# The transposes of a head's probabilities, one score tile later in the written order of attention

## The reference

```python
logits = [einsum('bqkgd,bskd->bkgqs', qi, ki) * scale for qi, ki in zip(qblk, ks)]
p = softmax(concatenate(logits))          # windowed heads: one sink logit more in the denominator
out = einsum('bkgqs,bskd->bqkgd', p, v)   # over latent keys and 128 past keys
```

## Time and profile before

| | us |
|---|---|
| median of 3 runs | 1852.12 (1851.22 to 1853.79) |
| the profiled execution | 1850.76 |
| its span, first to last instruction | 1849.0 |
| PE busy | 1738.5 (94%) |
| DVE busy | 1112.3 (60%) |
| ACT busy | 638.6 (35%) |
| attention of layer 0 | about 181 to 418 us of the span |
| attention of layer 1 | about 1082 to 1304 us of the span |

### The profile page before, as it was taken

One profiled execution on the slowest core, in us unless ns is written; L12 is line 12 of the kernel. 1 busy time (PEld: TensorE's weight loads), 2 busy tenths in 40 slices (PEclk: granted clock), 3 DMA queues, 4 the chain that ended last, 5 costly groups with the idle time before them and its releaser, 6 DMA issues.

```text
span 1849.0 us, 30546 instructions
## 1 busy us (share of the span) xinstructions
PE 1738.5 (94%) x11801; PEld 1563.9 (85%) x11801; DVE 1112.3 (60%) x2272; ACT 638.6 (35%) x1302; POOL 149.4 (8%) x152
## 2 busy tenths in 40 slices
PE   6999888889999999999999988879999999999997
PEld 4898555459999999999989965545899999999997
DVE  3656655554775656565772856656467665656575
ACT  2421553453432222223243235435344222222223
POOL 0351010101000000000003402010200000000000
PEclk7899999899999999999999999999999999999999
DMA  7431432233122222222222322202313222222221
GB/s 267 115 94 40 150 109 90 88 114 103 47 92 80 68 79 68 79 68 80 76 66 65 92 76 92 92 23 92 92 58 92 81 68 79 68 77 70 80 58 58
DMA packets 188441, 156.56 MB, mean 85 GB/s; under 512 B 7825, under 2 KB 175285, under 8 KB 188341
## 3 DMA queue, kind: packets, MB, share of 16 engines
q1 hardware_dynamic: 188340, 155.19, 27.4%
HBM read 151.86 MB, written 3.31 MB: 84 GB/s over the span
## 4 chain that ended last, share of the span: by engine, by line
PE 85%; DVE 7%; ACT 3%; issue 2%; DMA 1%; POOL 1%; SPq 0%; DVEq 0%; ACTq 0%
PE PS L1112 81%; PE PS L1116 5%; DVE QTR L1573 1%; DVE H_lo L1630 1%; POOL SS L764 1%; DVE H_lo L1876 1%; ACT PR L951 1%; DVE PR L1849 1%; DVE ST L1830 1%; ACT H_hi L783 1%; DMA RW<-in_w_in_dram 1%; DMA RW<-in_w_ada_dram 1%; DVE X L1679 0%; POOL W_lo L742 0%; ACT PT L783 0%
## 5 line engine op out<-in xcount | busy, mean ns | idle before, releaser
L1112 PE MATMUL PS<-H_hi,W_hi 128*128 128x384 f32 (+1 forms) x1728 | 416.6, 310 | 0.0
L1112 PE MATMUL PS<-H_hi,W_lo 128*128 128x384 f32 (+1 forms) x1728 | 416.5, 310 | 0.0
L1112 PE MATMUL PS<-H_lo,W_hi 128*128 128x384 f32 (+1 forms) x1728 | 416.5, 310 | 0.0
L1112 PEld LDWEIGHTS PS<-H_lo,W_hi 128*128 128x128 f32 x1728 | 275.7, 189 | 0.0
L1112 PEld LDWEIGHTS PS<-H_hi,W_lo 128*128 128x128 f32 x1728 | 275.5, 189 | 0.0
L1112 PEld LDWEIGHTS PS<-H_hi,W_hi 128*128 128x128 f32 x1728 | 274.5, 189 | 0.8 <-issue 0.8
L783 ACT ACTIVATE W_hi<-RW 128x1024 fp32r<-128x1024 f32 (+1 forms) x176 | 184.0, 1050 | 172.3 <-PE PS L1112 161.6
L1945 DVE TENSOR_SCALAR CF<-U,VT 128x644 f32<-128x644 f32 x88 | 48.9, 556 | 268.8 <-ACT U L783 268.6
L1112 PE MATMUL PS<-G_hi,W_hi 128*128 128x384 f32 (+1 forms) x704 | 171.5, 310 | 0.0
L1112 PE MATMUL PS<-G_lo,W_hi 128*128 128x384 f32 (+1 forms) x704 | 171.0, 309 | 0.0
L1112 PE MATMUL PS<-G_hi,W_lo 128*128 128x384 f32 (+1 forms) x704 | 170.8, 309 | 0.0
(11 more groups left out here) (168 smaller groups left out, 2467.7 us busy)
## 6 DMA issues: line engine op xcount, KB each, us to landing
RW<-in_w_ada_dram SPq DMA_DIRECT2D x96, 512.0 KB, 4.4
RW<-in_w_up_dram SPq DMA_DIRECT2D x88, 512.0 KB, 3.7
RW<-in_w_down_dram SPq DMA_DIRECT2D x44, 512.0 KB, 3.6
RW<-in_w_in_dram SPq DMA_DIRECT2D x28, 512.0 KB, 3.8
RW<-in_w_out_dram SPq DMA_DIRECT2D x16, 512.0 KB, 3.5
RW<-in_w_in_dram SPq DMA_DIRECT2D x8, 352.0 KB, 3.0
out_dram<-OUT SPq DMA_DIRECT2D x5, 512.0 KB, 2.9
XIN<-in_x_sample_dram SPq DMA_DIRECT2D x4, 512.0 KB, 6.4
```

What stands on the lines that cost most here:

```text
L1112: return nc.tensor.matmul(out, lhsT, rhs, start=start, stop=stop, skip_group_check=True)
```

## The change

Only the list changes. In the order of before, T("P",h,5) stood ahead of S(h+1,0), and the step T("P",h,k) behind S(h+1,k). Now T("P",h,5) stands behind S(h+1,0), T("P",h,k) behind S(h+1,k+1), and T("P",h,4), which no score tile is left for, behind the last SEL of the head, ahead of the next K or Q. The values follow: V(h,3) stands behind K, V(h,4) behind Q.

```diff
@@ -189,21 +189,22 @@
     for h in range(HEADS):
         t, v = probs(h - 1) if h else ([], [])
         if h == 8:
-            order += t[:1] + late + t[1:2]
+            order += late + t[:2]
             for x in range(2, len(t)):
                 order += v[x - 2:x - 1] + t[x:x + 1]
             order += v[-2:]
             t, v, late = [], [], []
+        order += late[:1]
         if h == 0 or kv_of(h) != kv_of(h - 1):
             order += [("T", ("K", kv_of(h), 0)), ("T", ("K", kv_of(h), 1))]
-        order += late + [("T", ("Q", h, 0)), ("T", ("Q", h, 1))]
+        order += late[1:2] + [("T", ("Q", h, 0)), ("T", ("Q", h, 1))] + late[2:]
         if h == 3:
             order.append(("PREP", 1))
         todo = [chunks.pop(0) for _ in range(1 + (len(chunks) > HEADS - h if h % 3 == 0 else len(chunks) >= 2 * (HEADS - h)))]
-        order += [("ADA", todo[0])] + t[:1]
+        order += [("ADA", todo[0])]
         for q in range(NQ):
             order.append(("S", h, q))
-            order += t[q + 1:q + 2] + v[q:q + 1]
+            order += t[q:q + 1] + (v[q - 1:q] if q else [])
             if q == 0:
                 order.append(("MOVE", todo[0]))
             if q == 1:
@@ -212,7 +213,7 @@
                 order += mla[3 * q:3 * q + 3]
             if q == 3 and len(todo) > 1:
                 order.append(("ADA", todo[1]))
-        late = v[5:]
+        late = t[5:] + v[4:]
         if len(todo) > 1:
             order += [("MOVE", todo[1]), ("SEL", todo[1])]
         if h == 7:
```

## The result

| | median us | runs | ratio to before, 95% |
|---|---|---|---|
| before, beside this set | 1852.95 (1851.22 to 1855.04) | 4 | |
| changed | 1870.34 (1867.35 to 1871.79) | 4 | 1.0091 (1.0074 to 1.0109) |
| changed, second set (experiment 5) | 1866.50 (1861.59 to 1867.41) | 4 | 1.0058 (1.0042 to 1.0075) |

The sign was right. The size was not: forecast 1862 with 1855 to 1869, and the first set lies above that range. The second set lies in it, and the two intervals hardly touch. So the question behind the result was what differs between executions of the same instructions. The chip of the first set is not on record, so a difference between chips is not ruled out; but the kernel before, on three chips, has means of 1855.0, 1855.8 and 1855.2, and the second set, on one chip, spreads over 5.8 us by itself.

What follows compares the result with a forecast made beforehand. PE was taken to bound the kernel (85% of the chain), so its idle time in attention counts in full. 9.6 + 1.6 - 1.0 = +10.2 us on the median of 1852.12 gave 1862, range 1855 to 1869.

Steps and rivals of the forecast that it cites:

- part 1: Ten head changes a layer: PE's wait for T("P",h,5) moves behind S(h+1,0), 31.2 us against 21.6 before, +9.6 us.
- the upper bound: Wait behind S(h+1,0): PE's first transpose after idle time or POOL's work beside DVE adds 0.3 us, so +15.5.
- part 2: T("P",h,4) behind SEL: K's second part waits 0.2 us for ACT's move at eight places, +1.6 us (0 to 2.5).
- part 3: Heads 7 to 8: T("P",6,4) and V(6,3) fill idle time, -0.5 us a layer, -1.0 in both (-2 to +1).
- The static sum: Whole kernel, without TensorE's clock: 9.6 + 1.6 - 1.0 = +10.2 us.
- TensorE's clock is left out of the sum: No clock loss counted, though one more dip at each of heads 0 to 1 and 8 to 9 would be +5.6 us.
- windows around a head start with a clock below 1: Sign of being wrong: around head starts TensorE is granted less than its full 2.4 GHz; no size given.
- the clock falls at every head: Rival: 20 clock dips of 1.4 us at head changes come on top, 1889 us; chance 0.07.
- The rival with the wait gone: DVE normalises (h,4) ahead of the new head's maximum, so all 21.6 us of wait are saved: 1831 us; chance 0.07.

Runs made afterwards that it cites:

- experiment 5: The changed kernel run again with only a comment altered, for a second set of runs and a second profile: median 1866.50 us, ratio 1.0058.
- Experiment 1: Changed kernel, but DVE normalises the old head's last tile before taking the new head's first maximum: median 1829.55 us, ratio 0.9865.
- experiment 2: Kernel before with only T("P",h,5) moved behind S(h+1,0), all other transposes and values left in place: median 1891.53 us, ratio 1.0205.
- experiments 7 and 11: Kernel of experiment 6 plus twelve unread matmuls in PE's waits between heads 7 and 8, run in two sets: medians 1822.59 and 1819.73 us.
- experiment 6: Kernel of Experiment 1 with T("P",h,4) ahead of the head's last SEL, except in head 7: median 1829.60 us, ratio 0.9863.
- second pair: Kernels of Experiment 1 and experiment 6, each run again on one chip: medians 1832.01 and 1828.41 us.

## Why the prediction was right or wrong

**Right, part 1.** That DVE takes the new maximum first and PE waits 1.59 us behind S(h+1,0) is measured to the hundredth: 1.59, 1.39 from head 3 to 4, 1.57 to 1.58 for windowed heads, against 1.59, 1.39 and 1.57. The 0.3 us more of the upper bound came at no place. The ten places of a layer sum to 19.8 - 2.2 - 1.95 = 15.65 (15.6 forecast). S(h+1,0) starts without a wait for `QTR`. Experiment 1 shows that this order on DVE is the cause, experiment 2 that moving T("P",h,5) alone brings it.

**Right, part 2.** K's second part waits 0.25 us at four places of a layer, 2.0 in both (1.6 forecast). SEL's wait is unchanged.

**Wrong, part 3.** The -0.5 us a layer did not come. PE's waits between heads 7 and 8 are 0.87 + 2.22 + 0.22 = 3.3 us in layer 0 and 1.31 + 2.20 + 0.22 = 3.7 in layer 1, against 2.49 + 0.48 + 0.23 = 3.2 and 2.65 + 0.94 + 0.22 = 3.8 before; in the second profile they are 3.6 and 3.8. So the term of -1.0 was in fact 0 to +0.3. Lines of the changed kernel's first profile, in both layers:

```profile
336.12 0.65 PE L1113 MATMUL PS<-PT,PMS 128*64 128x256 f32 x2 [0.87 <-ACT PT L784]
340.21 0.69 PE L1113 MATMUL PS<-PT,PMS 128*64 128x128 f32 x2
...
1239.65 0.65 PE L1113 MATMUL PS<-PT,PMS 128*64 128x256 f32 x2 [1.31 <-ACT PT L784]
1242.50 1.30 PE L1117 MATMUL PS<-K,PR 128*128 128x128 f32 x5 [2.20 <-DVE PR L1850]
```

Two of the kernel before, in layer 1:

```profile
1223.89 0.30 PE L1116 MATMUL PS<-K,PR 128*128 128x128 f32 x1 [2.65 <-DVE PR L1849]
...
1226.29 0.66 PE L1112 MATMUL PS<-PT,PMS 128*64 128x128 f32 x2 [0.94 <-DVE H_lo L1876]
```

V(7,5) starts 5.98 us after the last MLA product in layer 0 (340.21 - 334.23), where the five transposes ahead of it took 1.30 us, and 5.41 in the second profile, where they took 0.74: about the 5.3 to 5.9 forecast. In layer 1 it is 6.4 in both, as PE waits 1.3 us there for ACT's move before V(6,4). Besides, the first profile lost 5.1 us of clock in the 16 us from 336 on; the profile of before lost 3.4 in the 16 us from 328 on, the same place.

**Wrong: the clock, and a range too narrow for it.** The static sum was 10.2 and came out 12.1: part 3 is 1.0 to 1.3 of the difference, part 2 is 0.4, part 1 is 0.1. That alone would have left the result in the range. With the first set's mean of 1870.0 the forecast of 1862 misses 8. Of this 1.9 is the static part. 3.3 is the base: 1852.1 came from three runs, and 26 later runs of the kernel before have a mean of 1855.4. 2.2 is clock, 49.1 us lost in the first set against a mean of 46.9 before (in the second set it was 45.2). The 0.6 left over is rounding and the spread of the estimates. The 3.3 is probably clock as well: the profiled run of the base lost 40.7 us, the 26 lost 46.9 on average; the clocks of the two other runs of the base are not on record. So the failed step is "TensorE's clock is left out of the sum", with 3.7 us as what a measurement can tell and 1869 as the upper end. The eight runs of the changed kernel lie between 1861.6 and 1871.8, 10 us apart by where their clock falls, and the base was one execution at 0.978 and two more quick ones. On average the change cost no clock (47.1 us lost against 46.9), so the second set, at 1866.5, falls inside the range; which set came first was luck. Why the clock falls at a place in one execution and not in another stays open.

One of the prediction's signs of being wrong did appear: windows around a head start with a clock below 1, as at heads 0 to 1 of layer 0, 0.64 and 0.73 in the two profiles of the changed kernel. The rival "the clock falls at every head" did not happen in the changed kernel; experiment 2, with two waits around one tile, comes nearest to it. The rule of the Trainium skill ("TensorE: Matmul & The Clock Gate", Part 1) that recent activity sets the clock agrees with experiments 7 and 11. The unequal outcome of equal waits in the two profiles above, and experiment 6, with less idle time and less clock, are not explained by it alone.

The rival with the wait gone has its time from an order that the change did not make; experiment 1 made it: 1829.55 and 1832.01, where 1831 was worked out. The mechanism was as described, but the closeness is in part luck: at full clock 18.7 and 18.0 us are gained on the kernel before, not 21, and a better clock made up the rest.

## What to carry to other kernels

A wait moved behind other work is hidden only if what it waits for does not queue behind that same work on its own engine: look at how every engine walks the new order, not only at the one that waits. When independent work is put in front of a consumer, turn the producer's order too (here three lines, 1.7% less than the changed kernel at full clock and 1.0% less than the one before; 1.3% less than before in the medians). Before a forecast of half a per cent, find out how far runs of the unchanged kernel spread, and with what clock.

## What the runs showed of the hardware

- The same instruction stream, with the same wait for `PR` to a tenth of a microsecond, lost 25.6 and 15.3 us of granted clock in attention in two executions.
- Matmuls that compute nothing, placed in waits of 0.87 and 2.21 us, made the kernel of experiment 6 faster by 7.0 and 8.7 us in the median on two chips, although at full clock it was 0.7 and 2.1 us slower with them.
- Less idle time does not always mean more clock: with 10.6 us of waits removed (experiment 6 against 1) the mean granted clock went from 0.978 to 0.974, and from 0.977 to 0.974 in the second pair.
- From the end of a score tile of 128x640 to PE's next matmul that needed the old tile's probabilities took 1.59 us at twelve places of the changed kernel: 0.82 for DVE's reduction, 0.15 for the scaling, 0.29 for the multiplication of 128x128, the rest the reciprocal and the steps between engines.
